# Grouped-query attention scores: two matrix passes in place of three, with the low part of a query in the other head's rows

## The reference

```
qa = apply_axial_rope(rmsnorm(qa, q_norm_g), cos_a, sin_a)     # 512 tokens, 8 heads of 64
ka = apply_axial_rope(rmsnorm(ka, k_norm_g), cos_a, sin_a)     # 512 tokens, 2 key heads of 64
ya = blocked_attention(qa, ka, va, 1.0 / math.sqrt(64))

sc = einsum('bqhgd,bkhd->bhgqk', qblk, k) * scale
p = softmax(sc, axis=-1)
out = einsum('bhgqk,bkhd->bqhgd', p, v)
```

## Time and profile before

| what | value |
|---|---|
| median of 3 runs | 2858.58 us (2854.22 to 2861.07) |
| the profiled execution: its own time | 2862.51 us |
| the profiled execution: span from first to last instruction | 2860.70 us |
| PE busy | 98% of the span |
| DVE, ACT, POOL busy | 56%, 41%, 25% |
| mean granted TensorE clock | 0.993 of 2.4 GHz |
| grouped-query scores, layer 0 | 61.94 to 163.6 us |
| grouped-query scores, layer 1 | 854 to 956 us |

### The profile page before, as it was taken

The page is one execution under the profiler, slowest core; times in us unless marked ns, Lnnn a source line. Parts: engine busy times, 40 slices in busy tenths (PEclk is TensorE's granted clock), DMA queues, the critical chain, the costliest instruction groups (busy, mean ns, idle before and its releaser), DMA issues. The chain is left out here.

```text
span 2860.7 us, 34997 instructions
## 1 busy us (share of the span) xinstructions
PE 2789.8 (98%) x13382; PEld 2312.0 (81%) x13382; DVE 1598.3 (56%) x2159; ACT 1172.8 (41%) x1869; POOL 724.9 (25%) x607
## 2 busy tenths in 40 slices
PE   8999999999989999999999999999999999999998
PEld 6777888888877778888888788888888889888887
DVE  5787446334266884464543796555434568565532
ACT  4666334223246763342122655323233358432322
POOL 1564113314015741133041341122200014022211
PEclk9999999999999999999999999999999999999999
DMA  3011332232221113223222212233233210133232
GB/s 139 32 42 53 113 96 89 97 96 96 96 89 38 37 45 118 96 89 103 96 96 97 80 56 71 97 98 100 97 103 103 89 45 1 59 106 100 97 102 97
DMA packets 75127, 239.90 MB, mean 84 GB/s; under 512 B 9264, under 2 KB 17728, under 8 KB 74976
## 3 DMA queue, kind: packets, MB, share of 16 engines
q1 hardware_dynamic: 73776, 234.46, 24.7%
q0 software_dynamic: 928, 3.27, 0.4%
q10 hardware_dynamic: 272, 0.06, 0.0%
HBM read 232.51 MB, written 2.10 MB: 82 GB/s over the span
## 5 line engine op out<-in xcount | busy, mean ns | idle before, releaser
L1730 DVE TENSOR_TENSOR WL<-RAWW,WH 128x1024 fp32r<-128x1024 f32 (+3 forms) x429 | 577.5, 1349 | 735.3 <-ACT WH L1366 735.1
L2210 PE MATMUL bank<-UH,WH 128*128 128x512 f32 (+2 forms) x1968 | 768.8, 391 | 22.4 <-DVE UL L1747 11.5
L2212 PE MATMUL bank<-UH,WL 128*128 128x512 f32 (+2 forms) x1968 | 759.8, 386 | 0.0
L2211 PE MATMUL bank<-UL,WH 128*128 128x512 f32 (+2 forms) x1968 | 759.8, 386 | 0.0
L1366 ACT ACTIVATE WH<-RAWW 128x1024 fp32r<-128x1024 f32 (+3 forms) x432 | 432.7, 1012 | 398.7 <-DMA RAWW<-weights 398.1
L2210 PEld LDWEIGHTS bank<-UH,WH 128*128 128x128 f32 (+1 forms) x1968 | 371.5, 189 | 106.4 <-DVE UL L1747 15.1
L2211 PEld LDWEIGHTS bank<-UL,WH 128*128 128x128 f32 (+1 forms) x1968 | 371.7, 189 | 75.3 <-issue 2.7
L2212 PEld LDWEIGHTS bank<-UH,WL 128*128 128x128 f32 (+1 forms) x1968 | 371.5, 189 | 74.9
L2210 PE MATMUL bank<-HH,WH 128*128 128x512 f32 (+1 forms) x576 | 211.0, 366 | 0.0
L2211 PE MATMUL bank<-HL,WH 128*128 128x512 f32 (+1 forms) x576 | 210.6, 366 | 0.0
L2212 PE MATMUL bank<-HH,WL 128*128 128x512 f32 (+1 forms) x576 | 210.6, 366 | 0.0
(11 more groups left out here) (375 smaller groups left out, 4674.4 us busy)
## 6 DMA issues: line engine op xcount, KB each, us to landing
RAWW<-weights SPq DMA_DIRECT2D x432, 512.0 KB, 3.4
X<-x SPq DMA_DIRECT2D x8, 256.0 KB, 5.3
FF<-tables POOLq DMA_DIRECT2D x2, 1024.0 KB, 6.4
U<-S5U SPq DMA_DIRECT2D x32, 64.0 KB, 2.0
out<-FF SPq DMA_DIRECT2D x16, 128.0 KB, 1.8
GEL<-U SPq DMA_DIRECT2D x64, 16.0 KB, 1.8
S5B<-s_b POOLq DMA_DIRECT2D x1, 512.0 KB, 4.5
S5C<-s_c POOLq DMA_DIRECT2D x1, 512.0 KB, 4.0
```

Of the source, the lines that this page charges most:

```text
L1730: dve.tensor_tensor(slot_words(WL, c % SLOTS, size), slot_words(RAWW, c % SLOTS, size), f32(slot_words(WH, c % SLOTS, size)), ALU.subtract ...
L2210: nc.tensor.matmul(out_, w[0], x_[0], start=start, stop=False, **how)
L2211: nc.tensor.matmul(out_, w[0], x_[1], start=False, stop=False, **how)
L2212: return nc.tensor.matmul(out_, w[1], x_[0], start=False, stop=stop, **how)
```

## The change

For head 2i the rows of its partner in the query tile no longer hold the partner's high part but the low part of head 2i itself. The tile QH[:, i] now serves the even head only (rows 0 to 63 high, rows 64 to 127 low) and QL[:, i] the odd head only (rows 64 to 127 high, rows 0 to 63 low). The keys' high part stands in both halves of KH[:, k]; KL[:, k] keeps its zeros in the other half. One pass of such a tile with KH gives qh·kh + ql·kh, and one with KL gives qh·kl. The third pass goes. The copies and subtractions of a query tile, one of 128 rows each before, become two of 64 rows each; the high copies of the keys become four in place of two; POOL clears one tile in place of two.

```diff
@@ layer_inputs (POOL)
-                for v in (KH, KL):
-                    ins = pool.memset(f32(v[:]), 0.0)
-                ins.then_inc(k_zero, 1)
+                pool.memset(f32(KL[:]), 0.0).then_inc(k_zero, 1)
@@ rot_dest becomes rot_high and rot_low
+        HEAD_ROWS = [slice(k * HD, (k + 1) * HD) for k in range(KV_HEADS)]
+
+        def rot_high(st):
             if st.what == "q":
-                return [(QH[:, st.i, :], QL[:, st.i, :], slice(0, P))]
+                return [((QH, QL)[k][rows, st.i, :], rows) for k, rows in enumerate(HEAD_ROWS)]
             if st.what == "k":
-                halves = [slice(k * HD, (k + 1) * HD) for k in range(KV_HEADS)]
-                return [(KH[half, k, :], KL[half, k, :], half) for k, half in enumerate(halves)]
+                return [(KH[to, k, :], HEAD_ROWS[k]) for k in range(KV_HEADS) for to in HEAD_ROWS]
...
+        def rot_low(st):
+            if st.what == "q":
+                return [((QH, QL)[k][HEAD_ROWS[1 - k], st.i, :], (QH, QL)[k][rows, st.i, :], rows)
+                        for k, rows in enumerate(HEAD_ROWS)]
+            if st.what == "k":
+                return [(KL[rows, k, :], KH[rows, k, :], rows) for k, rows in enumerate(HEAD_ROWS)]
...
@@ turn_out (ACT)
-                    for h, _, rows in rot_dest(st):
+                    for h, rows in rot_high(st):
                         ins = act.activation(h, FF[rows, 6 + st.rot % 2, :], ACT.Copy)
@@ turn_low (DVE)
-                    for h, lo_, rows in rot_dest(st):
+                    for lo_, h, rows in rot_low(st):
                         ins = rest(lo_, FF[rows, 6 + st.rot % 2, :], h)
@@ att_scores (PE)
                     if st.h < HEADS:
-                        qs = QH[:, st.h // 2, q], QL[:, st.h // 2, q]
-                        ks = KH[:, st.h % 2, :], KL[:, st.h % 2, :]
+                        both = (QH, QL)[st.h % 2][:, st.h // 2, q]
+                        nc.tensor.matmul(BANK[2 + st.u % 2][:], both, KH[:, st.h % 2, :], start=True, stop=False)
+                        nc.tensor.matmul(BANK[2 + st.u % 2][:], both, KL[:, st.h % 2, :], start=False, stop=True
+                                         ).then_inc(scores.sem, 1)
```

More of the change, by code:

```diff
@@ L1349, in small_input @@
             return k, LP[:, l, G_CQ + k:G_CQ + k + 1]
-        def rot_dest(st):
+        HEAD_ROWS = [slice(k * HD, (k + 1) * HD) for k in range(KV_HEADS)]
+        def rot_high(st):
             if st.what == "q":
-                return [(QH[:, st.i, :], QL[:, st.i, :], slice(0, P))]
+                return [((QH, QL)[k][rows, st.i, :], rows) for k, rows in enumerate(HEAD_ROWS)]
             if st.what == "k":
-                halves = [slice(k * HD, (k + 1) * HD) for k in range(KV_HEADS)]
-                return [(KH[half, k, :], KL[half, k, :], half) for k, half in enumerate(halves)]
+                return [(KH[to, k, :], HEAD_ROWS[k]) for k in range(KV_HEADS) for to in HEAD_ROWS]
             if st.what == "mla":
-                return [(MQH[0:QK, st.h % 2, :], MQL[0:QK, st.h % 2, :], slice(0, QK))]
-            return [(MKH[HD:QK, k, :], MKL[HD:QK, k, :], slice(HD, QK)) for k in range(2)]
+                return [(MQH[0:QK, st.h % 2, :], slice(0, QK))]
+            return [(MKH[HD:QK, k, :], slice(HD, QK)) for k in range(2)]
+        def rot_low(st):
[4 more added lines that the diff above has]
+                return [(KL[rows, k, :], KH[rows, k, :], rows) for k, rows in enumerate(HEAD_ROWS)]
+            if st.what == "mla":
+                return [(MQL[0:QK, st.h % 2, :], MQH[0:QK, st.h % 2, :], slice(0, QK))]
+            return [(MKL[HD:QK, k, :], MKH[HD:QK, k, :], slice(HD, QK)) for k in range(2)]
         @block.scalar
@@ L2480, in step @@
                         ks = MKH[0:QK, i, :], MKL[0:QK, i, :]
-                    product(BANK[2 + st.u % 2][:], qs, ks, True, True).then_inc(scores.sem, 1)
+                        product(BANK[2 + st.u % 2][:], qs, ks, True, True).then_inc(scores.sem, 1)
                 elif kind == "att_transpose":
```

## The result

The changed kernel took **2871.27 us** (median of 7 runs, 2865.89 to 2873.78) against 2861.07 us for the kernel before on the same chip (7 runs). The ratio is **1.0031, 95% interval 1.0021 to 1.0042**: slower by 6 to 12 us, where the prediction said no change and put 0.11 on slower. The profiled execution has a span of 2870.7 us and a mean granted clock of 0.988 (before: 2860.7 us, 0.993).

What follows compares the result with a forecast made beforehand. PE, 98% busy, looked like the bound, but DVE ends its score-block waits and DVE and POOL are full in 132 to 142 us; -3.45 + 1.95 + 0.3 + 0.7 + 0.5 = 0.0 a layer, so 2858.6 us, range 2853.0 to 2864.0.

Steps and rivals of the forecast that it cites:

- A pass costs 0.23; 15 of 32 stay, -3.45 a layer: Score blocks: of 32 removed passes a layer, 0.23 us each, 15 save time and the rest lengthen PE's waits; -3.45 us.
- First score +1.95, wait 2.7: Ahead of each layer's first score: key copies +1.25, q0's second subtraction +0.7; PE's wait grows from 0.72 to about 2.7.
- Done just as DVE asks: Ahead of the first score: q0's second ACT copy ends at 62.27, just as DVE asks for it at 62.25.
- q3's second subtraction +0.7: At 133.5 us, where DVE and POOL are full: all 0.7 us of the added subtraction counts, per layer.
- upper bound of 1.7: q3's split subtraction, in the full DVE stretch: could cost up to +1.0 us on top of its 0.7.
- The sum without the clock, -0.5 a layer: Per layer, saved passes and additions without the clock term: -3.45 + 1.95 + 0.3 + 0.7 us.
- I take 0.5 a layer between 0 and 1.7: Clock term: a fall behind the first score's longer wait costs 0 to 1.7 us a layer; 0.5 taken.
- the range's clock term: Upper end of the range: the clock at its own bound adds 2 x 1.2 = +2.4 us over both layers.
- Rival 2: Slower by the clock: falls behind the first score's wait and the wait at 71.80, +4.6 a layer, 2867.8 us; chance 0.09.
- waits of up to 1.05 us: Argument against rival 2's second fall: such waits in the score blocks brought no fall in 132 to 142 us.
- PE busy down by 10 to 14 us: Sign of being right: PE's busy time drops some 10 to 14 us, its attention-stage waits growing by nearly as much.

Runs made afterwards that it cites:

- the passes alone: Kernel before without the pass of the keys with the query's low part in all 64 blocks, and without the additions: 2855.94 us, 0.9974 of before.
- the additions: Run alone: changed kernel with a third pass put back in all 64 blocks, leaving only the added ACT and DVE work: 2875.03 us, 1.0034 of before.
- both waits filled: Changed kernel with repeated passes in the waits ahead of each first score and near 136 and 931 us: 2866.28 us (1.0007), again 2869.46 (1.0034).
- the shared waits: Waits near 36, 830, 1614, 1640 us, filled with repeated passes: kernel before 2855.09 us (0.9982); changed, first-score waits filled too, 2855.98 (0.9987).

## Why the prediction was wrong, step by step

- *A pass costs 0.23; 15 of 32 stay, -3.45 a layer.* Right: -3.37 and -3.45 with the passes alone. The count holds wait by wait too: up to 71.80 that run has gained 0.26 (predicted 0.23), up to 83.36 0.95 (0.92), up to 106.35 1.62 (1.61), up to 130.64 2.79 (2.99), and nothing more up to 146.45.
- *First score +1.95, wait 2.7.* Nearly: 62.28 - 52.41 against 61.94 - 54.17 is +2.10, the wait 2.83. Key copies 1.26, second subtraction 0.65. "Done just as DVE asks" was 0.2 off: the subtraction started 0.83 behind the one ahead of it, when ACT's second copy had ended:

```profile
59.91 0.63 ACT L1472 ACTIVATE QL<-FF 64x512 fp32r<-64x512 f32 x1
```

```profile
59.81 0.69 DVE L1793 TENSOR_TENSOR CF<-bank,RSTD 128x512 f32<-128x512 f32 x1
60.64 0.69 DVE L1745 TENSOR_TENSOR QH<-FF,QH 64x512 fp32r<-64x512 f32 x1
61.34 0.69 DVE L1745 TENSOR_TENSOR QL<-FF,QL 64x512 fp32r<-64x512 f32 x1
```

 The pair's starts are 0.70 apart. That agrees with the Trainium skill, "VectorE: DVE Perf Modes", section "Two Vector instructions with no wait between them": where an input or output starts in another quadrant than the one before, the second is held until the first has finished. The pair at 60.39 and 61.00 in the earlier trace rows, with no such change, starts 0.61 apart.
- *q3's second subtraction +0.7.* Mis-sized: 1.90 in place of 0.60, +1.3, inside the upper bound of 1.7 that I gave. PE's wait behind it grew by 1.75 (0.41 to 2.16): 0.33 of that comes with the passes alone (0.74), the rest with the additions (1.83 with them alone, +1.42 in place of 0.7).
- *The sum without the clock, -0.5 a layer.* With both waits filled and no fall in the stages these take 104.22 and 104.23, +0.37 and +0.29; by span x clock the changed kernel is level with before. So the ledger of work was too low by 0.8 to 0.9 a layer, 0.6 of it q3's pair and 0.15 the first score; this is a small part of the 10 us.
- *"I take 0.5 a layer between 0 and 1.7."* **This step failed.** The clock took 8 to 12 us, not 1.0, and even the range's clock term was only 2.4 more. Within the stages the term was about right: in two of the three profiles of the changed kernel a fall costs 0.6 a layer (104.8 against 104.2), since the wait at 72 us behind it shrinks (0.55, where 1.69 stands without a fall). In the third a fall twice as long cost 1.9 in one layer and one behind the second wait 0.2 in the other (106.10 and 104.39). Wrong was to close the ledger at the stage's end. The larger part of the loss lies in falls elsewhere, above all in the state-space stage (+7.3 and +10.6 us between 1640 and 1720 in two profiles), which I had not looked at because nothing changes there. I also did not carry q3's pair through to PE's wait of 2.16, the second place of a fall.
- *Rival 2, 2867.8, 0.09.* The mechanism and nearly the size, but not by its sum: one fall a layer, not two, the second place 136 and 931 us and not 71.80 (where no profile of the changed kernel shows a fall, behind 0.55 to 1.7 us of wait), and most of the loss outside the stages. I argued against it with waits of up to 1.05 us, which said nothing of one of 2.16.
- *PE busy down by 10 to 14 us.* It went from 2789.8 to 2788.9. With the passes alone it is 2773.9, so they do take some 16 us out of PE's busy time; in the changed kernel the slower passes at the 1.2 GHz level fill that up.

**Shown:** the slowdown is granted clock and hardly work. At full clock both kernels are level within 2 us, and with PE's longer waits filled in both 0.9 us of the 10 is left (2856.0 against 2855.1). The two lengthened waits account for a part, 2.3 and 7.4 us by the ratios of two sets. **Open:** why the changed kernel meets the low clock in the state-space stage more often. Filling the shared waits takes that away, but which of them does it was not separated, so it is not shown how the change brings the loss about there; a later arrival alone (12 more passes in the kernel before) gave one slow profile, but not the loss on average. Near 443 us the changed kernel also waits 1.1 us longer, where ACT waits 1.22 us for a load of weights; no run tried this.

## What to carry to other kernels

Where PE has waits near 2 us, its granted clock is part of the ledger of the whole run, also in stages that the change does not touch: list every wait that the change makes longer than those after which the clock has stayed up, those behind a slower neighbour too, and take the price from repeated runs, since one profile and even one set of runs (1.0007, then 1.0034) is a draw. A wait that cannot be shortened can be filled with passes that the next product overwrites; in this kernel that was worth 6.1 us, about as much as leaving out the third pass alone (6.3). Splitting a 128-row vector instruction into two of 64 rows doubled its time here (0.63 each on ACT and 0.69 each on DVE, where the one took 0.63 and 0.68), so release the first half by itself if its reader needs no more.

## What was not expected of the hardware

- In the grouped-query score stages no wait of up to 1.83 us was followed by a fall; waits of 2.15 to 2.86 us were in some runs, not in others. Elsewhere shorter ones were: in four profiles the clock fell in the second attention near 251 us, behind a wait of 0.9, and in the changed kernel it fell at 807 us behind three of 0.86, 1.04 and 0.72 in a row. So the length of one wait alone does not tell whether a fall follows.
- The clock fell with PE never idle. In the kernel before the scores of the last attention (64 rows) start at 2309.59 and follow each other without a wait (PE is busy 3.30 of the 3.30 us from 2309.5, at a clock of 1.00), and then the 1.2 GHz level is there with PE busy for the whole window:

```profile
2309.59 0.50 PE L2210 MATMUL bank<-Q2H,K2H 64*128 64x512 f32 x1
...
2312.63 0.42 PE L2211 MATMUL bank<-Q2L,K2H 64*128 64x512 f32 x1
```

```profile
2313.00:2316.00 3.00, 3.00 (x12) 2.68 (x11) 2.50 (x6) 2.00 (x3) 0.00 (x0) 0.50 0.00 0
```
